# Earlier routing and row fetches in a PEER feed-forward, with half of each weight residual made on GpSimd

## The reference

```python
q = (x @ w_peer_q).reshape(T, 8, 128)                 # 8 heads
s1 = einsum('thd,kd->thk', q[..., :64], keys_1)       # 128 keys
s2 = einsum('thd,kd->thk', q[..., 64:], keys_2)
v1, i1 = top_k(s1, 16); v2, i2 = top_k(s2, 16)
cand = (v1[..., :, None] + v2[..., None, :]).reshape(T, 8, 256)
sc, ci = top_k(cand, 16)
e1 = take_along_axis(i1, ci // 16); e2 = take_along_axis(i2, ci % 16)
eidx = e1 * 128 + e2                                  # one of 16384 experts
gates = softmax(sc)
act = gelu(einsum('td,tkd->tk', x, peer_u[eidx]))     # 128 experts of each token
y = einsum('tk,tkd->td', gates * act, peer_v[eidx])
```

## Time and profile before

| | us |
|---|---|
| median of three runs | 3779.05 |
| the three runs | 3771.79, 3848.09, 3779.05 |
| profiled execution | 3809.69 |
| its span | 3807.6 |
| TensorE busy in the span | 3466.7 (91%) |
| VectorE busy | 2593.1 (68%) |
| ScalarE busy | 1788.6 (47%) |
| GpSimd busy | 1090.5 (29%) |

### The profile page before, as it was taken

One profiled execution on the slowest core, in us unless ns is written; L12 is line 12 of the kernel. 1 busy time (PEld: TensorE's weight loads), 2 busy tenths in 40 slices (PEclk: granted clock), 3 DMA queues, 4 the chain that ended last, 5 costly groups with the idle time before them and its releaser, 6 DMA issues. The chain is left out here.

```text
span 3807.6 us, 46395 instructions
## 1 busy us (share of the span) xinstructions
PE 3466.7 (91%) x17825; PEld 2940.0 (77%) x17825; DVE 2593.1 (68%) x3562; ACT 1788.6 (47%) x2344; POOL 1090.5 (29%) x646
## 2 busy tenths in 40 slices
PE   8999998779999999995996999799989997888899
PEld 5987887557878787784876767789989996776777
DVE  3463355468989898895345835468798996777784
ACT  3332342338888888886222322323337882222232
POOL 0001000037777777771000000000013444444430
PEclk9999678889999999997998969899999998999999
DMA  5453012247878777775211201325458999999995
GB/s 181 136 177 111 15 51 89 110 162 233 270 252 265 229 267 252 244 255 165 89 56 49 77 6 59 124 85 168 164 194 293 388 386 370 337 341 326 347 329 197
DMA packets 295195, 746.99 MB, mean 196 GB/s; under 512 B 53344, under 2 KB 158576, under 8 KB 260544
## 3 DMA queue, kind: packets, MB, share of 16 engines
q1 hardware_dynamic: 213744, 570.77, 42.2%
q0 software_dynamic: 81232, 173.25, 14.2%
HBM read 793.57 MB, written 110.65 MB: 237 GB/s over the span
## 5 line engine op out<-in xcount | busy, mean ns | idle before, releaser
L1832 DVE TENSOR_TENSOR w_lo<-w_raw,w_hi 128x2048 fp32r<-128x2048 f32 x288 | 659.0, 2289 | 116.0 <-ACT w_hi L1686 98.9
L1686 ACT ACTIVATE w_hi<-w_raw 128x2048 fp32r<-128x2048 f32 x288 | 550.7, 1913 | 29.8 <-DMA w_raw<-in_e_w,over_rows 28.4
L2816 POOL DMA_INDIRECT rows<-in_peer_u_rows,row_at x128 | 189.9, 1484 | 1298.7 <-DVE row_at L2972 1028.9
L1374 PE MATMUL ps_peer<-w_hi,coef_hi 128*128 128x512 f32 x768 | 312.0, 406 | 77.0 <-DVE w_lo L2902 52.4
L1374 PE MATMUL ps_peer<-peer_xT_hi,w_hi 128*128 128x384 f32 x1024 | 353.2, 345 | 16.6 <-DVE w_lo L2902 16.6
L588 DVE TENSOR_TENSOR w_lo<-w,w_hi 128x1024 fp32r<-128x1024 f32 (+5 forms) x138 | 172.7, 1262 | 265.2 <-ACT w_hi L574 264.3
L2027 PE MATMUL ps_gu<-w_hi,h2T_hi 128*128 128x512 f32 x792 | 323.5, 408 | 24.2 <-DVE w_lo L1832 24.0
L1375 PE MATMUL ps_peer<-peer_xT_lo,w_hi 128*128 128x384 f32 x1024 | 343.4, 335 | 0.0
L1376 PE MATMUL ps_peer<-peer_xT_hi,w_lo 128*128 128x384 f32 x1024 | 343.3, 335 | 0.0
L574 ACT ACTIVATE w_hi<-w 128x1024 fp32r<-128x1024 f32 (+5 forms) x138 | 148.9, 1088 | 402.0 <-DMA w<-in_w_in 227.8
L2902 DVE TENSOR_TENSOR w_lo<-w_raw,w_hi 128x2048 fp32r<-128x2048 f32 x128 | 292.7, 2287 | 56.9 <-ACT w_hi L2827 56.7
(11 more groups left out here) (526 smaller groups left out, 8469.2 us busy)
## 6 DMA issues: line engine op xcount, KB each, us to landing
w_raw<-in_e_w SPq DMA_DIRECT2D x195, 1024.0 KB
w_raw<-in_peer_u SPq DMA_DIRECT2D x64, 1024.0 KB
w_raw<-in_peer_v SPq DMA_DIRECT2D x64, 1024.0 KB
w<-in_w_in SPq DMA_DIRECT2D x60, 512.0 KB, 4.8
acts<-act_out SPq DMA_DIRECT2D x64, 384.0 KB
gates<-gate_tile SPq DMA_DIRECT2D x6, 4096.0 KB, 17.6
act_back<-acts SPq DMA_DIRECT2D x64, 384.0 KB
gates_back<-gates SPq DMA_DIRECT2D x64, 384.0 KB
```

Of the source, the lines that this page charges most:

```text
L1374: nc.tensor.matmul(out, w_hi, x_hi, start=first, stop=False)
L1686: nc.scalar.activation(w_hi[:, slot(n), :], w_raw[:, slot(n), :], ACT.Copy).then_inc(hi_done.sem, 1)
L1832: nc.vector.tensor_tensor(w_lo[:, slot(n), :], w_raw[:, slot(n), :], w_hi[:, slot(n), :].bitcast(F32), ALU.subtract).then_inc(lo_done.sem, 1)
L2816: nc.gpsimd.indirect_dma_start(out=row(i), out_offset=None, in_=src, in_offset=bass.IndirectOffsetOnAxis(ap=row_at[:, which, k:k + 1], axi ...
```

## The change

- The steps of routing are spread: each tile of 128 tokens is shifted, picked and divided as soon as its eight heads are ranked. Tile 0 in steps 5 to 10, tile 1 in 13 to 18, tile 2 in 21 to 26, one operation over 2048 elements a step (`pieces`), and tile 3 in steps 29 and 30 with three of them in each. `GATES_FROM` goes from 37 to 32, so gates are placed in steps 33 to 56 instead of 38 to 61.
- The list of sums is cut from 256 to 112: row i of the table of sums is kept whole for i below 4, and to its first 4 columns from there on. The table is written by two additions instead of one, and `pick` starts with ten small operations (`decode`) instead of four.
- Row fetches begin when tile 0 is routed, in step 10. `rows_at` gives the rows taken in each step of the first part: none to step 10, then 3 in a step without pieces, 1 in a step with one piece, 0 in a step with three. The 128 rows of `peer_u` are done in step 63. Those of `peer_v` are spread over steps 65 to 123, two or three a step (128 rows in 59 steps).
- In steps 5 to 32 (`SHARED` names the unit) VectorE makes the first half of the residual and GpSimd the second, each 1024 elements wide; TensorE waits for both. GpSimd issues this subtraction ahead of the row fetches of the step in its queue.

```diff
-KEY_STEPS = 28
-PICK_STEPS = 2 * T
-GATES_FROM = KEY_STEPS + PICK_STEPS + 1
+NPIECE = 6
+GATES_FROM = PH * T + 4 - FAST
 PER_STEP = 4
 NBATCH = SD // GB
 PER_CHUNK = CT // GB
 NROW = 8
-ROWS_FROM = GATES_FROM + 1
+GATES_TO = GATES_FROM + NBATCH // PER_STEP
+
+
+def ranked_at(t):
+
+    return PH * (t + 1) - FAST
+
+
+def pieces(step):
+
+    for t in range(T):
+        n = step - ranked_at(t) - 1
+        if t < T - 1 and 0 <= n < NPIECE:
+            return [(t, n)]
+        if t == T - 1 and 0 <= n < 2:
+            return [(t, i) for i in range(n * NPIECE // 2, (n + 1) * NPIECE // 2)]
+    return []
+
+
+def rows_at(step):
+
+    if step <= ranked_at(0) + NPIECE:
+        return 0
+    if step < GATES_FROM and pieces(step):
+        return 1 if len(pieces(step)) == 1 else 0
+    return 3
+
+
+def row_steps():
+
+    at = []
+    while not at or at[-1] < P:
+        at.append(min(P, (at[-1] if at else 0) + rows_at(len(at))))
+    at.append(P)
+    n, end = len(at), 2 * NG - 4
+    return at + [P + min(P, -(-P * (step + 1 - n) // (end - n))) for step in range(n, 2 * NG)]
+
+
+ROW_STEPS = row_steps()
+
+
+SHARED = range(FAST + 1, GATES_FROM + 1)
 
 
 def rows_by(step):
-
-    if step < NG:
-        return max(0, min(P, 4 * (step - ROWS_FROM + 1)))
-    dots = rows_by(NG - 1) + 3 * (step - NG + 1)
-    return dots if dots <= P else max(P, min(2 * P, dots - 3))
+    return ROW_STEPS[step] if step >= 0 else 0
 
 
 def rows_in(step):
     return range(rows_by(step - 1), rows_by(step))
...
+N_WIDE, N_SHORT = 4, 4
+NC = N_WIDE * PK + (PK - N_WIDE) * N_SHORT
...
+            def second_half_low(n):
+                pool.wait_ge(w_hi_done.sem, n + 1)
+                c = slice(W // 2, W)
+                nc.gpsimd.tensor_tensor(w_lo[:, n % NW, c], w[:, n % NW, c], w_hi[:, n % 2, c].bitcast(F32),
+                                        ALU.subtract).then_inc(pool_lo.sem, 1)
+
...
+            first = ranked_at(0) + NPIECE
+            for n in SHARED:
+                second_half_low(n)
+                if n == first + 1:
+                    pool.wait_ge(row_at_done.sem, 1)
+                    for i in range(NROW):
+                        fetch_row(i)
+                if n > first + 1:
+                    for i in rows_in(n - 2):
+                        fetch_row(i + NROW)
+            for i in range(rows_by(SHARED[-1] - 2) + NROW, 2 * P):
+                fetch_row(i)
+
...
-                nc.vector.tensor_tensor(w_lo[:, n % NW, :], w[:, n % NW, :], w_hi[:, n % 2, :].bitcast(F32),
+                c = slice(0, W // 2 if n in SHARED else W)
+                nc.vector.tensor_tensor(w_lo[:, n % NW, c], w[:, n % NW, c], w_hi[:, n % 2, c].bitcast(F32),
                                         ALU.subtract).then_inc(w_lo_done.sem, 1)
...
-                    nc.vector.tensor_tensor(cand[:], val[:, 0, :].unsqueeze(2).to_broadcast([P, PK, PK]),
-                                            val[:, 1, :].unsqueeze(1).to_broadcast([P, PK, PK]), ALU.add) \
-                        .then_inc(taken.sem, 1)
-
-            def shift():
-                key_round(NT)
-                for t in range(T):
-                    nc.vector.tensor_tensor(chosen[:, 2, t], best[:, t], best[:, t, :, 0:1].to_broadcast([P, PH, PK]),
-                                            ALU.subtract).then_inc(shifted.sem, 1)
-
-            def pick(t, j):
-                if j == 0:
-                    link(nc.vector.tensor_single_scalar(at[:, 0], best_at[:, t], 4, ALU.logical_shift_right))
-                    link(nc.vector.tensor_single_scalar(at[:, 1], best_at[:, t], PK - 1, ALU.bitwise_and))
-                    link(nc.vector.tensor_copy(atf[:], at[:]))
-                    link(nc.vector.tensor_copy(indexf[:], index[:, t]))
-                link(nc.vector.tensor_tensor(hot_flat, atf[:, j].rearrange("p h k -> p (h k)").unsqueeze(2)
-                                             .to_broadcast([P, PH * PK, PK]),
-                                             iota[:, 0:PK].unsqueeze(1).to_broadcast([P, PH * PK, PK]), ALU.is_equal))
-                link(nc.vector.tensor_tensor(hot[:], hot[:], indexf[:, j].unsqueeze(2).to_broadcast([P, PH, PK, PK]),
-                                             ALU.mult))
-                link(nc.vector.tensor_reduce(chosen[:, j, t], hot[:], AX, ALU.add))
+                    for lo, hi, n_j in ((0, N_WIDE, PK), (N_WIDE, PK, N_SHORT)):
+                        n_i, at_c = hi - lo, lo * PK
+                        ins = nc.vector.tensor_tensor(cand[:, at_c:at_c + n_i * n_j].rearrange("p (a b) -> p a b", b=n_j),
+                                                      val[:, 0, lo:hi].unsqueeze(2).to_broadcast([P, n_i, n_j]),
+                                                      val[:, 1, 0:n_j].unsqueeze(1).to_broadcast([P, n_i, n_j]), ALU.add)
+                    ins.then_inc(taken.sem, 1)
+
+            def shift(t):
+                nc.vector.tensor_tensor(chosen[:, 2, t], best[:, t], best[:, t, :, 0:1].to_broadcast([P, PH, PK]),
+                                        ALU.subtract).then_inc(shifted.sem, 1)
+
+            def decode(t):
+                nc.vector.tensor_copy(atf[:, 4], best_at[:, t])
+                nc.vector.tensor_copy(indexf[:], index[:, t])
+                nc.vector.tensor_single_scalar(at[:, 0], best_at[:, t], 4, ALU.logical_shift_right)
+                nc.vector.tensor_single_scalar(at[:, 1], best_at[:, t], N_SHORT - 1, ALU.bitwise_and)
+                nc.vector.tensor_single_scalar(at[:, 2], best_at[:, t], 2, ALU.logical_shift_right)
+                link(nc.vector.tensor_single_scalar(at[:, 3], best_at[:, t], PK - N_SHORT, ALU.bitwise_and))
+                link(nc.vector.tensor_copy(atf[:, 0:4], at[:, 0:4]))
+                nc.vector.scalar_tensor_tensor(atf[:, 0], atf[:, 2], float(N_WIDE * PK // N_SHORT - N_WIDE), atf[:, 0],
+                                               ALU.subtract, ALU.max)
+                link(nc.vector.scalar_tensor_tensor(atf[:, 3], atf[:, 4], float(N_WIDE * PK), atf[:, 3], ALU.is_lt,
+                                                    ALU.mult))
+                link(nc.vector.tensor_tensor(atf[:, 1], atf[:, 1], atf[:, 3], ALU.add))
+
+            def pick(t, piece):
+                j, part = divmod(piece, NPIECE // 2)
+                if piece == 0:
+                    decode(t)
+                if part == 0:
+                    link(nc.vector.tensor_tensor(hot_flat, atf[:, j].rearrange("p h k -> p (h k)").unsqueeze(2)
+                                                 .to_broadcast([P, PH * PK, PK]),
+                                                 iota[:, 0:PK].unsqueeze(1).to_broadcast([P, PH * PK, PK]), ALU.is_equal))
+                elif part == 1:
+                    link(nc.vector.tensor_tensor(hot[:], hot[:], indexf[:, j].unsqueeze(2).to_broadcast([P, PH, PK, PK]),
+                                                 ALU.mult))
+                else:
+                    link(nc.vector.tensor_reduce(chosen[:, j, t], hot[:], AX, ALU.add))
 
...
-            def divide():
-                dve.wait_ge(exped.sem, T)
-                link(nc.vector.tensor_reduce(gsum[:, 0], chosen[:, 2], AX, ALU.add))
-                link(nc.vector.reciprocal(gsum[:, 1], gsum[:, 0]))
-                nc.vector.tensor_tensor(own_gates[:].rearrange("p (h k) -> p h k", h=PH), chosen[:, 2, 0],
-                                        gsum[:, 1, 0].unsqueeze(2).to_broadcast([P, PH, PK]), ALU.mult)
-                for t in range(1, T):
-                    ins = nc.vector.tensor_tensor(chosen[:, 2, t], chosen[:, 2, t],
-                                                  gsum[:, 1, t].unsqueeze(2).to_broadcast([P, PH, PK]), ALU.mult)
-                ins.then_inc(chosen_done.sem, 1)
+            def divide(t):
+                dve.wait_ge(exped.sem, t + 1)
+                link(nc.vector.tensor_reduce(gsum[:, 0, t], chosen[:, 2, t], AX, ALU.add))
+                link(nc.vector.reciprocal(gsum[:, 1, t], gsum[:, 0, t]))
+                to = own_gates[:].rearrange("p (h k) -> p h k", h=PH) if t == 0 else chosen[:, 2, t]
+                ins = nc.vector.tensor_tensor(to, chosen[:, 2, t],
+                                              gsum[:, 1, t].unsqueeze(2).to_broadcast([P, PH, PK]), ALU.mult)
+                if t == T - 1:
+                    ins.then_inc(chosen_done.sem, 1)
 
...
-                elif n < KEY_STEPS:
+                elif n + FAST <= NT:
                     key_round(n + FAST)
-                elif n < KEY_STEPS + PICK_STEPS:
-                    if n == KEY_STEPS:
-                        shift()
-                    pick(*divmod(n - KEY_STEPS, 2))
-                    if n == KEY_STEPS + 1:
-                        find_rows()
-                    if n == KEY_STEPS + PICK_STEPS - 1:
-                        divide()
+                for t in range(T):
+                    if n == ranked_at(t):
+                        shift(t)
```

(32 more changed lines are left out.)

15 lines of the change are left out of this document (6 added, 9 removed).

## The result

| | before | after |
|---|---|---|
| median of 20 runs, us | 3771.94 | 3749.48 |
| lowest and highest | 3740.40, 3848.09 | 3716.89, 3767.41 |
| ratio (95% interval) | | 0.9945 (0.9927 to 0.9963) |
| span of the profiled execution | 3807.6 | 3742.1 |

The account below looks back on a forecast made before the run. It took DMA to bound the last part and TensorE most of the rest; 13 us (first part), 13 (between the parts) and 65 (last part, less 1) gave 90, from 3794 to 3704 us, range 3655 to 3760.

Parts of the forecast that it names:

- Bound of the last part: Last part, steps with three row fetches: DMA demand of 9.47 us a step against TensorE's 8.17.
- Size of the last part: Last part: moving row fetches out and spreading peer_v gains 65 us, bounds 38 and 80.
- The excess of 83 us: Last part, 52 steps: 508.2 us against 424.8 at 8.17 a step; 18 us of it expected to remain.
- The start of the sum: Whole kernel: gain subtracted from 3794 us, the median of all four times shown, giving 3704.
- The first rival: Last part: DMA stays the bound at 8.9 us a step, 42 us of excess kept; 3744 us, chance 0.20.
- Between the parts: TensorE's gap between first and last part: 11 us in place of 24, gain 13 us, bounds 8 and 17.
- First part: Steps before the gap: picks 15, first steps 4, lateness -4, start of row fetches -2, a gain of 13 us.
- the second rival: Steps 5 to 32: VectorE and GpSimd hold each other up, costing 43 us; 3747 us, chance 0.10.
- GpSimd's subtraction: GpSimd's half of the residual, 1024 numbers: 1.82 us each, from 7.29 us for 4096.
- 0 to 1 us: First part, 28 steps: the charge taken for GpSimd and VectorE hindering each other.
- The bound of 51 us from above: First part: most that GpSimd and VectorE hindering each other could cost, 1.82 us in each of 28 steps.
- The third rival: First part: TensorE waits for GpSimd's subtraction once it takes 4.3 us or more; gain gone at 7.6; chance 0.04.

Follow-up runs that it names:

- e5_no_burst: Changed kernel with the first eight row fetches split three, three and two, each behind a GpSimd half, instead of one run; ratio 0.9945, first part 641.6 us.
- e9_bunched: Changed kernel with the 128 rows of peer_v taken three a step from step 65, none behind; ratio 0.9969, last part 542.8 us.
- e3_no_half: Changed kernel with GpSimd's half not subtracted, ScalarE writing a plain copy of the weights there; ratio 0.9868, first part 618.1 us.
- e13_first_fetch: Changed kernel, whole residual on VectorE, rows re-planned, last-part fetches earlier, first two units' activations and gates fetched after step 60, not 62; 3686.18 us, ratio 0.9771.

## Why the prediction was right or wrong

**Bound of the last part: wrong, and the step that failed.** The prediction divided the busy time of DMA by the number of fetches, called the 9.47 us a step that it got a demand and set it against TensorE's 8.17. But 9.47 is only the share of 0.955 times the stretched step of 9.92, so a step stretched by any other wait, with packets under way, would have given much the same. A kernel with the same rows ran at 8.65 us a step once its fetches went out earlier, and with the rows of the change at 8.16 with no wait at all. The waits come from the gates' fetch, issued behind the refill at a step's end and slowed by the rows beside it. The change left that order alone, and the waits stayed.

**Size of the last part: 65 us forecast.** The traces give 529.6 and 538.1 after, against 571.2 and 539.6 before: 42 us from the profiled pair, 1.5 from the second pair, and 6 from the second trace of before to the mean of the two after (534). What is left of the measured 22 us for this part, with the first part's +6.4 and the 10.3 between the parts taken off, is 18. The excess of 83 us was itself a draw: 50 in the second trace. The prediction noted that its trace stood 31 us above the median and then read the excess from it in full. Of the 68 us by which 90 missed 22, this term holds 47, the first part 19 and the way between the parts 3.

**The start of the sum.** It subtracted the 90 us from 3794, the median of four times, of which two lay above 3800, where only one of 20 does; the median of 20 is 3772. So 3704 looks nearer to 3749 than the gain forecast deserves: 22 of the 68 us are made up by the start, and that is luck.

**The first rival** (DMA stays the bound) came near in outcome, with waits staying, a step of 8.8 to 9.0 us against its 8.9 and a time of 3744 us, and was wrong in mechanism. Its time is near partly by luck, as it too counts 13 us of gain in the first part.

**Between the parts: right.** 11 us of idle forecast, 13.88 measured; 13 us of gain forecast, 10.3 measured. The fetch took 12.4 us to the product, as assumed (13), but it went out at 3155.14, 3.1 us after step 62's end and not at it.

**First part: wrong in sign, by the second rival.** A gain of 13 us was forecast, 6.4 us were lost. Without GpSimd's subtraction the same plan takes 618.1 us, a gain of 18; so the sum of picks, key rounds and decoding was right, if anything shy, and the whole miss is GpSimd's subtraction: 24.3 us, of which about 0.8 is the run of fetches ahead of it and the rest that the two engines hold each other up. The step that failed was "0 to 1 us", with the argument that a late VectorE would have GpSimd's operation fall in its key round and be held up no further. But the key round ends in the additions of `cand`, which take two SBUF tiles, and these paid most. Nor was VectorE late now and then only: it was busy for 197.51 of 200.64 us. The bound of 51 us from above held, and the rival's 43 us was nearer than the forecast.

**GpSimd's subtraction: mis-sized.** 1.82 us, worked out from 4096 numbers; 2.39 measured in the median, up to 4.12 where it waited for VectorE. The third rival's threshold of 4.3 us was not reached.

**Smaller terms, near their forecast:** gate steps at 11.89 (nothing charged), the first four steps 6.1 us shorter (4 forecast), the run of eight fetches (2 us charged, 0.8 by `e5_no_burst`; step 12's own wait of 5.8 us was above the 0 to 4 allowed, but others take its place when it goes).

Not settled: how much of the 22 us is the last part's. It varies by 30 us between executions of one kernel, and two traces of each don't fix its mean; `e9_bunched`, with the changed first part and rows at three a step, is the nearest that was tried, and its ratios' intervals overlap with the changed kernel's. Nor was a run made with GpSimd's subtraction in place but reading nothing that VectorE competes for, so that they hold each other up rests on where the long operations start and end, and on `e3_no_half`.

## What to carry to other kernels

DMA engines that are busy at 95% are not yet a bound: issue the fetch that ends the wait earlier, with the same bytes, before moving bytes away from it. When work is handed to GpSimd, list VectorE's arithmetic on two SBUF tiles by the order in which it will meet GpSimd's, the short ones included: two additions of 64 and 48 numbers waited for up to 3.3 us. And when steps are cut at what a queue issues, check them against TensorE's own instructions, since the queue can be late too. Last, when the profiled execution stands far from the median, take a second trace before pricing a part that waits.

## What the runs showed of the hardware

- A subtraction of 1024 float32 numbers per partition takes GpSimd 2.35 us at the least, where three of 4096 had taken 7.29 each: 0.53 us more than a quarter of that.
- VectorE's max, find-index and match-replace operations kept their lengths beside GpSimd's subtraction: the find-index that ran inside one in step 22 took 0.26 us, and the longest of all over 112 numbers 0.27.
- The issue of one 1 MB fetch on SyncE took 7.90 us in `e13_first_fetch`, where it stood behind two fetches of activations and two of gates, 384 KB each. The weight fetch behind these four took 6.46 us in the kernel before and 1.6 to 2.7 in the other kernels made from the changed one; the median of the weight fetches is 0.38 us.
- The exponentials put tile by tile cost ScalarE a table load each time, and one to go back: nine loads of 1.28 us by step 33, where the kernel before had three. `e3_no_half` has them all, and its steps 5 to 26 take 8.75 us each.

```profile
L2899 ACT ACT_TABLE_LOAD x5 | 6.4, 1283 | 0.1
L2939 ACT ACT_TABLE_LOAD x4 | 5.1, 1283 | 0.1
```
